# Output projections with plain f32 operands inside the attention blocks, with the next norm row by row behind them

## What is computed

```python
h = rms_norm(x, attn_norm); q, k, v = split(h @ w_in)          # 4 pairs of causal heads, 4 "diff" heads
x = x + mixed @ w_out                                           # mixed: the normed attention outputs, 1024 wide
x = x + peer_ffn(rms_norm(x, ffn_norm))                         # routing to 16 of 16384 experts in 8 heads
x = x + (dilated_attention(rms_norm(x, g0)) * silu(gate)) @ a_w_out   # mixer a: 3 dilation groups
x = x + (grid_attention(rms_norm(x, g1)) * silu(gate)) @ b_w_out      # mixer b: 2-D neighbourhoods
```

## Time and profile before

| what | value |
|---|---|
| median of three executions | 1697.78 us |
| profiled execution, its own time | 1696.35 us |
| its span, first to last instruction | 1694.6 us |
| PE busy | 1551.4 us, 92% of the span |
| DVE busy | 1062.8 us, 63% |
| ACT busy | 722.7 us, 43% |
| mean granted PE clock | 0.961 |
| DMA moved | 239.34 MB |

### The profile page before, as it was taken

The page is one execution under the profiler, slowest core; times in us unless marked ns, Lnnn a source line. Parts: engine busy times, 40 slices in busy tenths (PEclk is TensorE's granted clock), DMA queues, the critical chain, the costliest instruction groups (busy, mean ns, idle before and its releaser), DMA issues. The chain is left out here.

```text
span 1694.6 us, 29111 instructions
## 1 busy us (share of the span) xinstructions
PE 1551.4 (92%) x8931; PEld 1373.0 (81%) x8931; DVE 1062.8 (63%) x2585; ACT 722.7 (43%) x1570; POOL 44.6 (3%) x44
## 2 busy tenths in 40 slices
PE   6995799999998999999999999789999997869987
PEld 3663599888887888999999999689999997668885
DVE  4676579977776776666666666645555554366663
ACT  2442341222223444444444444345555554345552
POOL 0000061000000000000000000000000000000000
PEclk9997899999999999999999999889999998879997
DMA  8300243432225555555555555374444441085410
GB/s 343 112 1 1 81 154 120 150 111 88 92 76 198 194 190 190 184 193 182 192 182 190 185 186 187 123 273 137 137 138 138 146 146 30 1 281 146 119 27 25
DMA packets 162635, 239.34 MB, mean 141 GB/s; under 512 B 41728, under 2 KB 91392, under 8 KB 161664
## 3 DMA queue, kind: packets, MB, share of 16 engines
q1 hardware_dynamic: 162560, 238.42, 43.2%
HBM read 237.09 MB, written 1.29 MB: 141 GB/s over the span
## 5 line engine op out<-in xcount | busy, mean ns | idle before, releaser
L191 PE MATMUL experts_acc<-experts_uh,experts_wh 128*128 128x512 f32 x512 | 201.1, 393 | 5.8 <-DVE experts_ul L1682 5.8
L192 PE MATMUL experts_acc<-experts_ul,experts_wh 128*128 128x512 f32 x512 | 200.8, 392 | 0.0
L193 PE MATMUL experts_acc<-experts_uh,experts_wl 128*128 128x512 f32 x512 | 199.7, 390 | 0.0
L1173 PE MATMUL plain_u<-ffn_h,down_raw 128*128 128x256 f32 x832 | 192.1, 380 | 1.8 <-ACT early L1576 1.4
L1655 ACT ACTIVATE experts_uh<-ffn_h 128x512 fp32r<-128x512 f32 x256 | 147.3, 624 | 82.8 <-PE experts_acc L193 75.1
L193 PE MATMUL projection<-hT_high,down_low 128*128 128x256 f32 x608 | 172.1, 283 | 0.0
L192 PE MATMUL projection<-hT_low,down_high 128*128 128x256 f32 x608 | 172.0, 283 | 0.0
L191 PE MATMUL projection<-hT_high,down_high 128*128 128x256 f32 x608 | 171.7, 282 | 0.0
L1173 PEld LDWEIGHTS plain_u<-ffn_h,down_raw 128*128 128x128 f32 x832 | 152.3, 190 | 22.6 <-issue 4.7
L1682 DVE TENSOR_TENSOR experts_ul<-ffn_h,experts_uh 128x512 fp32r<-128x512 f32 x256 | 165.0, 685 | 3.3 <-ACT experts_uh L1655 3.3
L191 PE MATMUL mix_a_pj<-mix_a_wh,hT_high 128*128 128x384 f32 x384 | 136.6, 356 | 17.0 <-DVE mix_a_wl L566 17.0
(11 more groups left out here) (308 smaller groups left out, 3129.6 us busy)
## 6 DMA issues: line engine op xcount, KB each, us to landing
down_raw<-in_downT SPq DMA_DIRECT2D x256, 256.0 KB, 3.4
ffn_h<-in_up SPq DMA_DIRECT2D x256, 256.0 KB, 2.8
mix_a_w_raw<-in_wa SPq DMA_DIRECT2D x48, 768.0 KB, 6.1
block_w_raw<-in_w SPq DMA_DIRECT2D x16, 768.0 KB, 7.1
mix_b_w_raw<-in_wb SPq DMA_DIRECT2D x16, 768.0 KB, 6.9
route_raw<-in_route SPq DMA_DIRECT2D x16, 576.0 KB, 3.8
wo<-in_wo SPq DMA_DIRECT2D x2, 2048.0 KB, 15.1
mix_a_w_raw<-in_wa SPq DMA_DIRECT2D x16, 256.0 KB, 3.4
```

The lines of the kernel that those rows point to most:

```text
L191: pe.matmul(out, lhs[0], rhs[0], start=start, stop=False, skip_group_check=True)
L192: pe.matmul(out, lhs[0], rhs[1], start=False, stop=False, skip_group_check=True)
L193: return pe.matmul(out, lhs[1], rhs[0], start=False, stop=stop, skip_group_check=True)
L1173: mm = pe.matmul(self.u[b][:, 0:SEQ], self.raw[b][:, k, :], self.h[:, k, :], start=k == 0, stop=k == KD - 1, skip_group_check=True)
```

## The change

- Each of the three projections moves into its attention block. Its operands are plain f32: `keep_y` writes yT in one operation, and wo is used as it was loaded. 32 matmuls of 512 columns stand in place of 96 passes.
- Some of the 32 are placed in PE's program in slots of the tail, by the tables FILLS (the first index counts steps behind the last pair, the second is the slot): 19 in block1, 13 in mix_a, 5 in mix_b. They are those of the first six rows k, for which y is ready by then. The others (13, 19, 27) stand behind the last y transposes, token half 0 first. The banks are those of the block (pj, xp, sc), each free after a wait that stands in `project`.
- The next norm follows in the same block (for block1 and mix_a), one token half after the other: square on ACT, root and scaling on DVE, transposes, windows. mix_b's block stores each half of x as soon as it is added.
- The blocks project1 to project3, norm1, norm3 and the store are gone. norm2 stays.
- Route: pieces 0 and 1 are both plain and come from the down_raw buffers, which block1 loads at its end; the four raw buffers are loaded from the route block's start, and down_raw's first chunks when products 0 and 1 are done.
- mix_b's first two weight pieces are loaded at the end of mix_a's loads, into the buffers shared with mix_a; its gate piece is loaded at mix_b's start, ahead of wob and the bias tiles.

```diff
+FILLS_1 = {(0, 0): 1, (0, 1): 1, (0, 3): 5, (0, 4): 2, (0, 5): 1, (1, 0): 2, (1, 1): 1, (1, 3): 6}
+FILLS_A = {(0, 0): 1, (0, 1): 3, (0, 3): 2, (0, 4): 1, (0, 5): 2, (0, 8): 1, (0, 10): 1, (0, 12): 1, (1, 0): 1}
+FILLS_B = {(0, 1): 2, (0, 4): 1, (0, 7): 1, (0, 11): 1}
...
+        acc = [pj[0][:], pj[1][:], xp[:].rearrange("p t a c -> p (t a c)"), sc[:, 0:512]]
+        n_early = sum(fills.values())
+        in_tail = [(k, b) for k in range(KD - 2) for b in range(2)] + [(k, b) for b in range(2, 4) for k in range(KD - 2)]
+        in_tail = in_tail[:n_early]
+        at_end = [(k, b) for b in range(4) for k in range(KD) if (k, b) not in in_tail]
+        turned_banks = [v.rearrange("p (k t) -> p k t", k=4) for v in (pt[:], sc[:, 512:], pj[0][:], pj[1][:])]
...
             if finish is not None:
+                if gated:
+                    sp.wait_ge(lows, n_pairs * ring * PARTS)
                 finish(sp)
+            if out is not None:
+                for t in range(NT):
+                    sp.wait_ge(x_added, 2 * t + 2)
+                    sp.dma_start(out[:, t, :], x[:, t, :]).then_inc(stored, 16)
+                sp.wait_ge(stored, 16 * NT)
...
+            def project(k, b):
+
+                if k == 0:
+                    if b < 2:
+                        pe.wait_ge(evicted, n_pairs * nq)
+                        if gated:
+                            pe.wait_ge(silu_ready, n_pairs)
+                    elif b == 2:
+                        pe.wait_ge(qk_ready, n_pairs * groups)
+                    else:
+                        pe.wait_ge(biased, before(n_pairs))
+                pe.wait_ge(wo_landed[k // 4], 16)
+                pe.wait_ge(y_ready, k + 1)
+                t, h = b // 2, b % 2
+                mm = pe.matmul(acc[b], yT[:, k, t * P:(t + 1) * P], wo[:, k, h * 512:(h + 1) * 512], start=k == 0, stop=k == KD - 1,
+                               skip_group_check=True)
+                if k == KD - 1:
+                    mm.then_inc(projected, 1)
...
+                    if isinstance(p, int) and p >= n_pairs:
+                        at = sum(fills.get((a, b), 0) for a in range(2) for b in range(SLOTS_STEP) if (a, b) < (p - n_pairs, s))
+                        for k, b in in_tail[at:at + fills.get((p - n_pairs, s), 0)]:
+                            project(k, b)
             in_steps(pe, step)
+            for k, b in at_end:
+                project(k, b)
+            if after is not None:
+                for t in range(NT):
+                    if t == 0:
+                        pe.wait_ge(pts_ready, before(n_pairs))
+                        pe.wait_ge(biased, before(n_pairs))
+                    pe.wait_ge(next_h_ready, t + 1)
+                    for k in range(KD):
+                        mm = pe.transpose(turned_banks[2 * t + k // 4][:, k % 4, :], next_h[:, t, k * P:(k + 1) * P], ident[:])
+                        if k % 4 == 3:
+                            mm.then_inc(next_turned, 1)
...
+            if after is not None:
+                for t in range(NT):
+                    act.wait_ge(x_added, 2 * t + 2)
+                    act.activation(next_h[:, t, :], x[:, t, :], ACT.Square, accum_out=next_sum[:, t:t + 1]).then_inc(next_summed, 1)
+                for n in range(2 * NT):
+                    act.wait_ge(next_full, n + 1)
+                    act.activation(window(after["hT"][0], n), window(after["full"], n), ACT.Copy).then_inc(next_high, 1)
...
-                    dve.scalar_tensor_tensor(tiled(yf[:]), tiled(yp, flip), 0.5, tiled(silu[qb][:]), ALU.mult,
-                                             ALU.mult).then_inc(y_ready, 1)
+                    y, silu_y = tiled(yp, flip), tiled(silu[qb][:])
+                    into = tiled(yT[:, q, :])
+                    if by_residue:
+                        into = yT[:, q, :].rearrange("p (i t r) -> p t r i", t=NT, r=RES // NT)
+                        y, silu_y = [v.rearrange("p t (r i) -> p t r i", r=RES // NT) for v in (y, silu_y)]
+                    dve.scalar_tensor_tensor(into, y, 0.5, silu_y, ALU.mult, ALU.mult).then_inc(y_ready, 1)
                 else:
                     at = COLUMNS["o_moba"] + q
-                    dve.tensor_scalar(yf[:], yp, cons["columns"][:, at:at + 1], None, ALU.mult).then_inc(y_ready, 1)
-                dve.drain()
-                yh, yl, yv = yT[0][:, q, :], yT[1][:, q, :], yf[:]
-                if by_residue:
-                    yh, yl = [v.rearrange("p (i r) -> p r i", r=RES) for v in (yh, yl)]
-                    yv = yv.rearrange("p (r i) -> p r i", r=RES)
-                dve.tensor_copy(yh, yv)
-                dve.drain()
-                dve.tensor_tensor(yl, yv, yh.bitcast(F32), ALU.subtract)
...
+                    dve.tensor_scalar(yT[:, q, :], yp, cons["columns"][:, at:at + 1], None, ALU.mult).then_inc(y_ready, 1)
...
+            def add(b):
+                t, h = b // 2, slice(b % 2 * 512, b % 2 * 512 + 512)
+                dve.wait_ge(projected, b + 1)
+                dve.tensor_tensor(x[:, t, h], x[:, t, h], acc[b], ALU.add).then_inc(x_added, 1)
+
+            def next_scaled(t):
+                dve.wait_ge(next_summed, t + 1)
+                dve.drain()
+                inverse_root(dve, *[v[:, t:t + 1] for v in (next_r, next_sum)], D, *[v[:, t:t + 1] for v in (next_hm, next_a, next_b)])
+                dve.tensor_scalar(next_h[:, t, :], x[:, t, :], next_r[:, t:t + 1], None, ALU.mult).then_inc(next_h_ready, 1)
+
+            def next_window(n):
+                b = n % 2
+                dve.wait_ge(next_turned, n + 1)
+                dve.tensor_tensor(window(after["full"], n), turned_banks[n], after["gain"][:, 4 * b:4 * b + 4].unsqueeze(2).broadcast_to([P, 4, P]),
+                                  ALU.mult).then_inc(next_full, 1)
+
+            def next_low(n):
+                dve.wait_ge(next_high, n + 1)
+                dve.tensor_tensor(window(after["hT"][1], n), window(after["full"], n), window(after["hT"][0], n).bitcast(F32), ALU.subtract)
+            add(0)
+            add(1)
+            if after is not None:
+                next_scaled(0)
+            add(2)
+            add(3)
+            if after is not None:
+                next_window(0)
+                next_window(1)
+                next_scaled(1)
+                next_low(0)
+                next_low(1)
+                next_window(2)
+                next_window(3)
+                next_low(2)
+                next_low(3)
...
+            for b in range(NW):
+                sp.dma_start(raw[b][:], weights[b]).then_inc(landed[b], 16)
+            for b in range(2):
+                sp.wait_ge(q_ready, b + 1)
+                ahead.load(sp, b, b)
...
-                if isinstance(hp, int) and hp == 0:
+                if isinstance(hp, int) and hp < 2:
                     return
                 for h in range(2):
                     k = slice(KD // 2 * h, KD // 2 * (h + 1))
-                    pool.wait_ge(w_highs, hp * 2 + (h - 1))
+                    pool.wait_ge(w_highs, hp * 2 + (h - 3))
...
-                first = isinstance(hp, int) and hp == 0
+                first = isinstance(hp, int) and hp < 2
                 if first:
-                    pe.wait_ge(landed[b], 16)
+                    pe.wait_ge(first_landed[b], 16)
                 for k in range(KD):
                     if first:
-                        mm = pe.matmul(qp[b % 2][:, 0:SEQ], raw[b][:, k, :], ahead.h[:, k, :], start=k == 0, stop=k == KD - 1,
+                        mm = pe.matmul(qp[b % 2][:, 0:SEQ], ahead.raw[b][:, k, :], ahead.h[:, k, :], start=k == 0, stop=k == KD - 1,
...
+                def finish_first(sp):
+                    for b in range(2):
+                        sp.dma_start(down_raw[b][:], d["route"][b][:, 0:KD, :]).then_inc(first_landed[b], 16)
                     sp.wait_ge(stored, 32)
                     sp.wait_ge(late, 32)
                 attention_phase(nc, "block1", pieces, n_pairs=8, kinds=["causal"] * 4 + ["diff"] * 4, groups=1, hT=whole, yT=yT,
-                                cons=sbt, minus_lam=sbt["minus_lam"][:], ahead=store_pad, finish=scratch_kept)
-                project_phase(nc, "project1", yT, wo, landed, x)
-        if start < 2 <= upto:
+                                cons=sbt, minus_lam=sbt["minus_lam"][:], ahead=store_pad, finish=finish_first, x=x, wo=wo,
+                                wo_landed=landed, fills=FILLS_1, after={"gain": column("ffn", KD), "full": whole, "hT": hT})
...
+                                finish=load_pieces_b, x=x, wo=wo, wo_landed=landed, fills=FILLS_A,
+                                after={"gain": column("mix_b", KD), "full": whole, "hT": hT})
...
-                    pieces_b.load(sp, 0, 0, 0)
-                    pieces_b.load(sp, 1, 1, 0)
+                def load_last(sp):
                     pieces_b.load_gate(sp, 0)
+                    load_wo(sp)
```

206 lines of the change are left out of this document (83 added, 123 removed).

## The result

| | before | after |
|---|---|---|
| median | 1698.59 us (4 runs) | 1650.04 us (3 runs, 1648.15 to 1656.07) |
| ratio, 95% interval | | 0.9721, 0.9683 to 0.9759 |
| profiled execution | 1696.35 us, span 1694.6 | 1656.07 us, span 1653.9 |
| the same kernel once more, with other runs of before | 1696.41 us | 1651.30 us (1651.04 to 1652.72), ratio 0.9733, 0.9717 to 0.9749; span 1650.9 |

The account below looks back on a forecast made before the run. TensorE, busy 1551.4 of 1694.6 us, waits in the tails' serial chains at a low clock. Gains 17.9 + 16.5 + 7.4 + 6.2 = 48.0, less 2.1, gave 1650.5, at the median 1651.9; own range 1643 to 1660, wider 1642 to 1669.

Parts of the forecast that it names:

- The price of a plain matmul: In the projections: one plain f32 matmul of 512 columns takes 0.865 us at full clock, 1.73 at 1.2 GHz.
- The seams: From each block's last y transpose to the next block's first product, or the end: 19.4, 15.1 and 6.4 us shorter.
- Why the tails are shorter: In the last pairs: full clock and shorter keep_y outweigh delays from fills; block1's last y transpose at 166.9 against 167.44.
- keep_y: Between the seams: keep_y loses 0.87 us of DVE per pair, giving 4.5 us in mix_b, 1.7 in block1, nothing in mix_a.
- Route: In the route block: 0.65 us lost on weights 1, 1.4 (bounds 0 and 5) on the late weight 4 reload; 2.0 together.
- First bias tile: At mix_b's start: the gate's 0.5 MB ahead in SP's queue makes the tile 1.3 us later, bounds 0 and 1.4.
- Slow starts: Long matmul streams behind each y may begin at 1.2 GHz: 0.7 us lost each, 2.1 in all, bounds 0 and 1.7 each.
- fills displace the chain: In the tails: ready transposes wait behind the 37 fills, costing up to 32 us; half of that gives 1668; chance 0.15.
- clock lost in the last tail: In mix_b's tail: PE's clock is not held despite five fills, costing 7 us, total 1659; chance 0.12.
- loads take over: In route and at mix_b's start: pieces or bias tiles land late, costing 5 and 6 us, total 1660; chance 0.08.
- The fourth: From last pairs to projection ends: PE stays at 1.2 GHz, 96 matmuls cost 83 us more, total 1735; chance 0.02.
- fifth: In the tails: holes stay empty as fills wait until the chain's end; 32 and 4 us lost, total 1688; chance 0.03.

Follow-up runs that it names:

- fills done twice: Changed kernel with fills kept in the tails, but all 32 projection groups run again behind each last y transpose, the fills' results thrown away: 1680.43 us, ratio 0.9906.
- the heavier one: Changed kernel with a cast and a subtraction put back into each keep_y, on buffers nobody reads: 1654.95 us, ratio 0.9755.
- the last experiments: Changed kernel with bias tiles loaded before output weights (1652.20 us), or output weights later in mix_b (1651.11), also in mix_a with route reordered (1646.67), then in halves (1641.24).

## Why the prediction was right, point by point

The terms of the sum, as lengths between marks (forecast; measured in the two executions of the change; all against the one trace of before):

| | forecast | measured |
|---|---|---|
| opening | none | +1.4, +1.1 |
| block1 with its tail | -2.2 | -1.3, -1.3 |
| y to route | -19.4 | -19.5, -19.6 |
| route | +2.0 | +7.8, +2.7 |
| spread, experts | none | +0.7, +1.0 |
| mix_a with its tail | -2.7 | -3.0, -2.7 |
| y to mix_b | -15.1 | -14.9, -14.9 |
| mix_b with its tail and the bias wait | -4.2 | -4.4, -2.5 |
| y to the end | -6.4 | -7.5, -7.5 |
| streams starting at 1.2 GHz | +2.1 | none |
| sum | -45.9 | -40.7, -43.7 |

- **The price of a plain matmul** held: 0.44 us a record in the seams, 0.84 a matmul by the fills done twice, for a forecast of 0.865 from a form of half the width.
- **The seams** held within 0.4 us but for the last (6.4 forecast, 7.5 measured; its 27 matmuls at 0.84 and not 0.865 are 0.7 of the 1.1). Block1's last y transpose fell at 167.69 for 166.9, with an opening that took 1.4 us more; the route block started at 189.07 for 188.6.
- **Why the tails are shorter** was half wrong. In block1 the q/k transposes come 1.3 us later behind the last product than without fills, and 0.9 later than before (forecast 0.6); the full clock gives most of it back, and the tail is 0.4 longer than without fills. The transposes came at 151.16 and 150.83, outside the 1 us around 149.70 that was named as a sign. In mix_a's tail the held clock is worth 3.2 us. In mix_b's the fills push the chain back by 1.8 to 2.5 us net, and the tail is shorter than before by 0.6 (13.7 against 14.3) for 1.0 forecast.
- **keep_y**: 4.5 us in mix_b and 1.7 in block1 forecast, about 4 and 1 by the heavier one. (Five waits that fall by at most 0.87 give 4.35 at most, so the 4.5 was a little more than its own source allows.) In mix_a nothing, as priced.
- **Route**, the mis-sized step: "I put the stall at 1.4, bounds 0 and 5". In the second execution the wait was 1.2 us and the whole give-back 2.7. In the profiled one it was 3.6, with some 2.5 us of half clock behind it, together 7.8, beyond the 0.65 + 5 of the bounds; a wait of over 3 us for route_w_low was also one of the prediction's own signs of being wrong. The bounds had the wait but not the low clock that was seen behind it. Nor was a slow start priced: the first 9.3 us of the route block ran at a clock of 0.70 and 0.69 in the two executions, 0.82 in the same stretch before. That is an estimated 1.1 us (0.12 of 9.3), and with it the sum for the second execution is 0.65 + 1.2 + 1.1 = 2.95, for the measured 2.7.
- **First bias tile**: 1.3 us later forecast; the wait grew from 7.29 to 9.36 in one execution and to 8.5 in the other, 2.1 and 1.2.
- **Slow starts**: 2.1 us forecast, none seen; the windows behind each y transpose stand at 1.00, where the kernel without fills has 0.93 behind the first and seams 5.5 us longer than with the fills done twice. This is the larger part of what the held clock brings; the forecast counted a loss instead.
- **The total** is partly luck. By spans the gain is 40.7 and 43.7 for 45.9; what came out worse (opening, block1, route, spread and experts) is partly made up by the slow starts that did not come and by the 1.1 us more at the end. The medians fell by 45 and more because the traced execution of before (1696.35) lies below its median and those of the change (1656.07, 1652.72) are the longest of the runs they belong to.

Of the rivals, the first (fills displace the chain) is out for mix_a, whose tail they shorten, and for block1 but for 0.4 us net; for mix_b's five fills it came true, with 1.8 to 2.5 us of the 4.2 that they hide. The second (clock lost in the last tail) came about in one of eleven traces with fills there, for 1.7 us. Whether those fills are what holds the clock there is open: without them this tail stood at 1.00 in one trace and at 0.86 (0.72 and 0.85 in the windows above) in the other. The Trainium skill (TensorE: Matmul & The Clock Gate, Part 4: PE-mode transpose) says that transposes don't count as activity as matmuls do; no run here tests it. The third (loads take over) is what the last experiments are about: true of mix_b's start, but the waits were there before the change too. The fourth and fifth are excluded by the clock and by the kernel without fills.

Left open: 0.7 to 1.0 us more in spread and experts, which the change does not touch, and the 1.7 us by which the opening differs between executions.

## What to carry to other kernels

Independent matmuls put into the holes of a serial chain are worth their own length, plus what the held clock saves in the chain and in the stream behind it, less what they push the chain back where a hole is shorter than they are. A kernel that runs the filler and then throws it away gives the first; beside the kernel without filler it gives the other two only as one net sum, and the timeline of each hole is needed to part them. A large transfer that is not needed soon cost its wait at each of the three places in the queue that were tried; sending half of it much later removed the hole. Forecast a late landing together with the clock that can fall behind the wait.

## What was not expected of the hardware

- One wait of 3.6 us in the route was followed by a stretch at half clock (0.50 over 210 to 214 us), and the same kernel with a wait of 1.2 us stayed at 1.00: 5.1 us between two executions of the same kernel, with a wait 2.4 us longer.
- After the same 1.2 us of idle PE, the same four records took 3.65 us in one execution and 1.96 in another (clock 0.57 and 1.00).
- At mix_b's start 4 MB of output weights cost the same whether they stood ahead of the bias tiles, behind them, or behind two pairs of loads (1651.3, 1652.2 and 1651.1 us). With mix_a's and the route's edits beside it, sending the second half behind the seventh pair gave 5.4 us more (1646.7 to 1641.2).
- The last tail ran at 1.00 without any fills in one trace, at 0.86 without them in another, and at 1.00 in ten of eleven with them.
